# Two output projections of a transformer kernel: three matmuls per weight tile become two, one of them 512 columns wide

## The reference, cut to what matters

```python
for l in range(DEPTH_2):
    x = x + hybrid_mixer(rms_norm(x, norm_mix[l]), w_in[l], ..., w_out[l], rows, cos, sin)
    x = x + memory_cross_attention(rms_norm(x, norm_mem_q[l]), rms_norm(mem, norm_mem_kv[l]), ...)
    x = x + conv_ffn(rms_norm(x, norm_ffn[l]), w_up[l], conv_w[l], conv_b[l], w_down[l])
return rms_norm(x, norm_final)
```

## Time and profile before

| | |
|---|---|
| median of 3 runs | 2555.58 us (2552.3 to 2555.68) |
| profiled execution, its own time | 2551.63 us |
| its span | 2549.8 us |
| mean granted TensorE clock | 0.962 |
| busy: TensorE, VectorE, ScalarE, POOL | 92%, 61%, 48%, 24% |
| matmuls from L729 with rounded weights | 6688 + 3424 + 3424 + 1632, 275 to 300 ns each in flight |
| DMA | 342.94 MB, 134 GB/s on average |

### The profile page before, as it was taken

One profiled execution on the slowest core, in us unless ns is written; L12 is line 12 of the kernel. 1 busy time (PEld: TensorE's weight loads), 2 busy tenths in 40 slices (PEclk: granted clock), 3 DMA queues, 4 the chain that ended last, 5 costly groups with the idle time before them and its releaser, 6 DMA issues. The chain is left out here.

```text
span 2549.8 us, 47516 instructions
## 1 busy us (share of the span) xinstructions
PE 2338.9 (92%) x19162; PEld 2195.9 (86%) x19162; DVE 1566.3 (61%) x2510; ACT 1215.1 (48%) x1859; POOL 621.2 (24%) x744
## 2 busy tenths in 40 slices
PE   4999999899999898799989899996898998889998
PEld 3888999798998687699977789995698998778998
DVE  4665654645654665465546656546667975656994
ACT  4455544444543642455345554443445554444653
POOL 3114211013211030032121132213174540053550
PEclk8889999999999999899999999998999999989999
DMA  4223545323555221155442245453243554233554
GB/s 160 84 83 133 180 154 189 123 83 122 176 162 169 100 68 51 51 168 179 155 144 84 90 136 173 160 189 121 83 163 120 189 165 166 67 119 130 189 171 136
DMA packets 52715, 342.94 MB, mean 134 GB/s; under 512 B 5888, under 2 KB 7104, under 8 KB 20160
## 3 DMA queue, kind: packets, MB, share of 16 engines
q1 hardware_dynamic: 51984, 336.26, 39.9%
q0 software_dynamic: 560, 4.26, 0.4%
HBM read 339.38 MB, written 1.05 MB: 134 GB/s over the span
## 5 line engine op out<-in xcount | busy, mean ns | idle before, releaser
L729 PE MATMUL ps<-arena_r,ring_hi 128*128 128x272 f32 (+1 forms) x6688 | 1605.5, 289 | 15.6 <-DVE arena L2107 7.4
L729 PEld LDWEIGHTS ps<-arena_r,ring_hi 128*128 128x128 f32 x6688 | 1178.2, 192 | 19.9 <-DVE arena L2107 7.8
L729 PE MATMUL ps<-y_r,ring_hi 128*128 128x272 f32 (+1 forms) x3424 | 1024.5, 299 | 22.7 <-POOL arena_r L2843 10.2
L1983 DVE TENSOR_TENSOR ring_lo<-ring,ring_hi 128x2048 fp32r<-128x2048 f32 (+1 forms) x348 | 737.8, 2121 | 411.8 <-ACT ring_hi L1461 411.0
L729 PE MATMUL ps<-y_r,ring_lo 128*128 128x272 f32 (+1 forms) x3424 | 989.1, 289 | 0.0
L729 PEld LDWEIGHTS ps<-y_r,ring_hi 128*128 128x128 f32 x3424 | 659.8, 193 | 59.1 <-issue 25.6
L1461 ACT ACTIVATE ring_hi<-ring 128x2048 fp32r<-128x2048 f32 (+1 forms) x348 | 607.5, 1747 | 121.9 <-DMA ring<-dn 49.9
L729 PEld LDWEIGHTS ps<-y_r,ring_lo 128*128 128x128 f32 x3424 | 661.7, 193 | 0.0
L729 PE MATMUL ps<-arena_r,ring_lo 128*128 128x272 f32 (+1 forms) x1632 | 469.2, 287 | 0.0
L729 PEld LDWEIGHTS ps<-arena_r,ring_lo 128*128 128x128 f32 x1632 | 311.3, 191 | 0.0
L1461 ACT ACTIVATE arena<-arena 128x272 f32<-128x272 f32 (+7 forms) x199 | 93.4, 472 | 409.5 <-DVE arena L2538 268.8
(11 more groups left out here) (229 smaller groups left out, 1725.8 us busy)
## 6 DMA issues: line engine op xcount, KB each, us to landing
ring<-gu SPq DMA_DIRECT2D x88, 1024.0 KB, 5.0
ring<-dn SPq DMA_DIRECT2D x64, 704.0 KB, 4.0
ring<-up SPq DMA_DIRECT2D x44, 1024.0 KB, 5.1
ring<-fox_in SPq DMA_DIRECT2D x32, 1024.0 KB, 5.1
ring<-sdn SPq DMA_DIRECT2D x32, 704.0 KB, 4.0
ring<-gdn_in SPq DMA_DIRECT2D x16, 1024.0 KB, 5.1
ring<-in SPq DMA_DIRECT2D x16, 1024.0 KB, 5.1
ring<-gla_in SPq DMA_DIRECT2D x12, 1024.0 KB, 5.1
```

Of the source, the lines that this page charges most:

```text
L729: return nc.tensor.matmul(dst, w, mv, start=start, stop=stop)
L1983: V.tensor_tensor(ring_lo[:, slot, 0:w], ring[:, slot, 0:w], ring_hi[:, slot, 0:w].bitcast(F32), ALU.subtract).then_inc(lo_ready, 1)
```

## The change

The input of a chunk becomes one view of its high and its low part, 2 x 256 columns (h2_both_r, a_both_r), and one matmul takes both through the high weights into a PSUM tile of 512 columns, which is a whole bank. The low weights by the high input go as a second matmul of 256 columns to the first half of that tile. In sdn the high input lies first in memory, so the first half collects both products of the high input and the second half high weights by low input; in out2 the low part lies first, so the halves are the other way round for the wide matmul. Each tile thus holds two partial sums of 256 columns, and residual() adds first the one half to x, waits for that, then adds the other. This holds for out2_0, out2_1, sdn0 and sdn1. No other stage, no transfer and no weight split changes.

```diff
--- before.py
+++ after.py
@@ -525,6 +525,7 @@
         h1_r, h1_lo_r = view_r(0, FC, T), view_r(7104, FC, T)
         h2_r, h2_lo_r = view_r(5120, FC, SEQ), view_r(10752, FC, SEQ)
         y_lo_r, y_lo2_r = view_r(18304, KC, T), view_r(18176, KC, SEQ)
+        h2_both_r, a_both_r = view_r(5120, 2, FC, SEQ), view_r(14080, 2, KC, SEQ)
         a_hi_r, a_o_r = view_r(16128, KC, SEQ), view_r(14080, KC, SEQ)
         m_lo_r, m_y_r, m_hi_r = view_r(7168, KC, SEQ), view_r(11264, KC, SEQ), view_r(17152, 4, SEQ)
 
@@ -728,7 +729,7 @@
             def mm(dst, w, mv, start=True, stop=True):
                 return nc.tensor.matmul(dst, w, mv, start=start, stop=stop)
 
-            def blocks(nb, tpb, kc, src, width, ready, after=None, banks=BANKS, middle=None):
+            def blocks(nb, tpb, kc, src, width, ready, after=None, banks=BANKS, middle=None, double=False):
 
 
 
@@ -750,10 +751,15 @@
                                 pe.wait_ge(lo_ready, i * (2 * turn) + (2 * (n.block + b) + half + 1))
                             hi, lo = ring_hi[:, slot, at:at + P], ring_lo[:, slot, at:at + P]
                             shi, slo = src(k)
-                            dst = acc(n.tile + t, width, P, banks)
-                            mm(dst, hi, shi, k == 0, False)
-                            mm(dst, hi, slo, False, False)
-                            last = mm(dst, lo, shi, False, k == kc - 1)
+                            if double:
+
+                                mm(acc(n.tile + t, 2 * SEQ, P, banks), hi, shi, k == 0, False)
+                                last = mm(acc(n.tile + t, SEQ, P, banks), lo, slo, False, k == kc - 1)
+                            else:
+                                dst = acc(n.tile + t, width, P, banks)
+                                mm(dst, hi, shi, k == 0, False)
+                                mm(dst, hi, slo, False, False)
+                                last = mm(dst, lo, shi, False, k == kc - 1)
                             if tpb == 1 and k == kc // 2 - 1:
                                 last.then_inc(mid_ready, 1)
                             if middle is not None and k == kc // 2 - 1:
@@ -964,13 +970,13 @@
                 all_read()
                 n.out += KC
 
-            def project_out(nb, tpb, kc, src, width, chunks, late):
+            def project_out(nb, tpb, kc, src, width, chunks, late, double=False):
                 def ready(k):
                     if k >= late:
                         pe.wait_ge(late_split, n.late + k - late + 1)
                     else:
                         pe.wait_ge(out_split, n.split + k + 1)
-                blocks(nb, tpb, kc, src, width, ready)
+                blocks(nb, tpb, kc, src, width, ready, double=double)
                 n.split += late
                 n.late += chunks - late
                 new_norm(width)
@@ -1427,7 +1433,7 @@
                     blocks(nb, tpb, kc, y_parts2, SEQ, y_chunk)
                     n.pair += FC
                 elif name.startswith("sdn"):
-                    blocks(nb, tpb, kc, lambda k: (h2_r[:, k, :], h2_lo_r[:, k, :]), SEQ, lambda k: pe.wait_ge(h_split, n.pair - FC + k + 1))
+                    blocks(nb, tpb, kc, lambda k: (h2_both_r[:, :, k, :], h2_r[:, k, :]), SEQ, lambda k: pe.wait_ge(h_split, n.pair - FC + k + 1), double=True)
                     new_norm(SEQ)
                 elif name.startswith("dn"):
                     w = SEQ if name == "dn3" else T
@@ -1436,7 +1442,7 @@
                 elif name.startswith("in2"):
                     hybrid(name, nb, tpb, kc)
                 elif name.startswith("out2"):
-                    project_out(nb, tpb, kc, lambda k: (a_hi_r[:, k, :], a_o_r[:, k, :]), SEQ, KC, KC)
+                    project_out(nb, tpb, kc, lambda k: (a_both_r[:, :, k, :], a_hi_r[:, k, :]), SEQ, KC, KC, double=True)
                 elif name.startswith("memkv"):
                     memory(name, nb, tpb, kc)
                 elif name.startswith("memq"):
@@ -2013,12 +2019,17 @@
                     v.wait_ge(sqsum_ready, n.norm * KC + c)
                     V.tensor_tensor(sqsum[:, 0:width], sqsum[:, 0:width], sq[:, c % 2, 0:width], ALU.add).then_inc(sqsum_ready, 1)
 
-            def residual(dst, width, norm_width, hook, short):
+            def residual(dst, width, norm_width, hook, short, double):
 
                 for c in range(KC):
                     if short:
                         hook(c)
-                    V.tensor_tensor(dst[:, c, :], take(c, width), dst[:, c, :], ALU.add).then_inc(evacuated, 1)
+                    if double:
+
+                        step(V.tensor_tensor(dst[:, c, :], take(c, 2 * SEQ)[:, 0:SEQ], dst[:, c, :], ALU.add))
+                        V.tensor_tensor(dst[:, c, :], take(c, 2 * SEQ)[:, SEQ:2 * SEQ], dst[:, c, :], ALU.add).then_inc(evacuated, 1)
+                    else:
+                        V.tensor_tensor(dst[:, c, :], take(c, width), dst[:, c, :], ALU.add).then_inc(evacuated, 1)
                     if not short:
                         hook(c)
                     if c:
@@ -2723,7 +2734,7 @@
                     n.out += 4
                 if name in GAINS:
                     second = name.startswith(("out2", "memo", "sdn"))
-                    residual(xs if second else x, SEQ if second else T, SEQ if second or name == "dn3" else T, after, tpb == 1)
+                    residual(xs if second else x, SEQ if second else T, SEQ if second or name == "dn3" else T, after, tpb == 1, name.startswith(("out2", "sdn")))
                     if name == "dn3":
 
                         V.memset(u_gp[:, :, 0:1], 0.0)
```

## The result

The changed kernel takes 2557.9 us (median of 22 runs, 2552.28 to 2568.61), the kernel before 2552.41 us (22 runs, 2541.86 to 2556.59). The ratio is 1.0025, with a 95% interval from 1.0013 to 1.0036: slower by a quarter of a per cent, a little more than the 0.2% that the prediction took as its bound, which the interval includes. The forecast was a gain of 0.14%. The time lies inside the range (2547 to 2558), by a hair; the direction was wrong.

What follows compares the result with a forecast made beforehand. TensorE's matmul spacing was taken to bound out2 and sdn. 4.5 us saved there less 0.9 us lost in two tails gave -3.6 us, from the median 2555.58 to 2552.0 us (-0.14%), range 2547 to 2558.

Steps and rivals of the forecast that it cites:

- The bound: In out2 and sdn TensorE's matmul spacing is the time: 117.8 ns per 256 columns in sdn, 353.4 per step.
- A gap per matmul and not per column: In out2 and sdn, wide matmul takes its columns plus one 11.1 ns gap, 224.4 ns; a step saves 11.1.
- rival 1: In out2 and sdn the gap is per column: wide matmul 235.6 ns, saved 0, 2556.5 us; chance 0.24.
- The 4.5 us saved: TensorE in out2 and sdn: 402 paying steps x 11.1 ns = 4.5 us saved.
- Rival 2: In out2 and sdn the wide matmul hides the next weight load: 215.6 ns, 2548.5 us; chance 0.15.
- Rival 3: In out2 and sdn the wide matmul is dearer than two: 243 ns, +3.9 us, 2559.5 us; chance 0.10.
- Steps that don't pay: Of 480 steps, 12 at out2's 1.2 GHz starts, 44 in sdn's second tiles, 22 at sdn0's end save nothing.
- Inside the stages it is covered.: In out2 and sdn the added 0.46 us of VectorE per tile is hidden; out2 busy about 16.3 of 20.35 us.
- bound for lost cover: In out2, if cover were gone, a tile would cost up to 0.46 us, 7 us over 16 tiles.
- After out2, memkv works on other data for 22 us and hides it.: Behind out2, the last tile's later residual costs nothing, since memkv runs on other data for 22 us.
- Two tails: At the ends of sdn0 and sdn1 the second addition is exposed: 2 x 0.46 = 0.9 us lost.
- The sum: Whole kernel: -4.5 + 0.9 = -3.6 us, giving 2552.0 us, -0.14%; forecast's chance 0.47.

Runs made afterwards that it cites:

- e7: Kernel before with 224 instead of 256 columns in every sdn matmul, one execution, trace only: matmuls start 111.7 ns apart.
- e6: Kernel before with the sum-of-squares matmul moved behind memkv's third tile, one execution, trace only: memkv0 27.06, memkv1 25.27 us.
- e10: Kernel before with the edits of e6 and e9 together: ratio 1.0044 (1.0028 to 1.0060).
- e13: As e9 on the kernel before, but the second half of the split also waits for POOL's last y step: 2549.04 against 2553.49 us, 0.9985 (0.9970 to 0.9999).
- e2: Changed kernel with the wide matmul but one VectorE addition per tile, second half left out of the sum: 2552.25 us, ratio 0.9993 (0.9977 to 1.0010).
- e11: Kernel before with two idle extra VectorE additions at every out2 tile, one execution, trace only: memkv0 28.81, memkv1 28.52 us.
- e1: Kernel before, three matmuls kept, with an idle second VectorE addition per tile in out2 and sdn: 2558.09 against 2551.0 us, ratio 1.0023 (1.0010 to 1.0036).
- e3: Kernel before with the change made in out2 alone, sdn as before: 2555.51 us, ratio 1.0014 (0.9999 to 1.0028).
- e8: Changed kernel with sdn's wide matmul reading 512 adjacent columns, low input left out, one execution, trace only: seven sdn1 tiles 54.66 us.
- e9: Kernel before, last residual and sums put ahead of the second half of the next weight split in one-tile-per-block stages: ratio 1.0001 (0.9989 to 1.0014).

## Why the prediction was wrong, point by point

- **The bound.** Right for the time inside the stages: TensorE's matmuls bound out2 and sdn, before and after. But behind TensorE in out2 stood a loop of VectorE and ScalarE that was slower than it even before, and the prediction did not see it.
- **"A gap per matmul and not per column", 224.4 ns for the wide matmul.** Wrong. It takes 233.4, and the narrow one behind it 120.0: rival 1 (twice the old matmul, nothing saved) holds to a tenth of a nanosecond per step. The 4.5 us saved were 402 times a gap that one instruction less does not remove. The rows had both readings, 1.066 against 1.063 for a rate, and I chose by the 0.9 ns that up0 lies lower. Rival 2 fell with it: a wide matmul over the next load took 233.4 ns and not 215.6. The Trainium skill (TensorE: Matmul & The Clock Gate, LDWEIGHTS) gives a load the time of its columns over 1.2, 106.7 ns for 128 columns, an estimate from that page; the 111.7 ns in e7 lie near it, and no run here shows that the load sets them. Rival 3 fell too, the slope of 0.49 ns per column did not carry to 512. What the 11.1 ns are stays open: in sdn1 of e6, e10 and e13 they are 6.7, with the same matmuls.
- **Steps that don't pay** (start at 1.2 GHz, second tile, end of sdn0). They never mattered, since no step paid.
- **"Inside the stages it is covered."** Wrong, and this makes the loss. The busy time of VectorE in out2 was about as forecast (15.3 of 20.4 us at the full clock in the changed kernel, 16.3 of 20.35 forecast), and it hid nothing: what counted was the turn-taking of two queues, VectorE's and ScalarE's, 5.85 us per two tiles before and 6.31 after, where TensorE needs 5.65. I named who stands behind the residual and did not add up their chain. The prediction had a bound for lost cover, 7 us over out2's 16 tiles, and gave it no place in the sum and no rival of its own.
- **"After out2, memkv works on other data for 22 us and hides it."** Wrong in its place: TensorE's queue holds the sum of squares behind memkv's first tile, 3 us after out2, not 22. These two steps together are 1.81 + 2.22 us in memkv, of which 0.8 to 1.1 and 2.2 are left at the next sdn, where the sum had nothing.
- **Two tails, 0.9 us.** Right after sdn1, 0.46 us by the traces. After sdn0 the two traces differ by 0.1 us, which is less than such traces differ by themselves. The times resolve neither.
- **The sum.** 0 saved, 3.0 to 3.3 us lost behind out2, 0.6 in tails: 3.6 to 3.9 us by the traces. The medians give 5.5, the ratio 6.4 with an interval from 3.3 to 9.2. The traces reach only its lower end; what the rest is, a share of the clock or chance, stays open. That the time fell into the range at all is luck: two steps were wrong, and rival 1's 2556.5 us, from which the upper end was drawn, had no loss in memkv. Slower by over 0.2% had a chance of 0.08, since all mechanisms for it but a dearer wide matmul were taken as covered.

## What to carry to other kernels

A busy share of 64% (VectorE in out2 before) says nothing about cover where two in-order engines release each other tile by tile: add up one round of their chain (who waits for whom, in queue order) and compare that with the time of the engine that should bound. For a stage's last product, look in the bounding engine's own queue for the first entry that needs it; that entry, and not the next stage that reads it, sets how late it may be. And before fewer, wider matmuls are bought with work elsewhere, run the wide matmul by itself, as e2 does: two widths 16 columns apart left both readings open, and e2 decides it.

## What the runs showed of the hardware

- Rounded (float32r) matmuls at the 2.4 GHz level started 0.456 to 0.462 ns per column apart at 256, 272 and 512 columns, where the clock alone gives 0.417; at the 1.2 GHz level 256 columns took 213.3 ns, exactly the clock's, and fp32 matmuls of 272 columns at 2.4 GHz took 229 ns, where twice the columns are 226.7. At 224 columns the spacing was 111.7 ns. In sdn1 of three traces (e6, e10, e13) 256 columns took 113.4 ns instead of 117.8. What limits the spacing, and what chooses between these two, is not shown by any run here.
- Joining two matmuls of 256 columns on the same weights into one of 512 left the step at 353.4 ns (233.4 + 120.0 against 3 x 117.8).
- After a TensorE wait of 3.8 us in memkv0 of e11 (3.7 in memkv1) the granted clock was 0.50 for 3.41 us; after waits of 1.5 to 2.2 us in after, e1 and e3 it stayed at 1.00, and after one of 2.19 us in e8 it fell for 3.41 us.
- A POOL step of 0.48 us took 2.51 us when it began just after a VectorE subtraction of two 2048-column operands of 2.29 us, and 0.48 us again when it was kept apart; TensorE's wait behind it was 2.31 us in e9 and 0.34 in e13. The Trainium skill (SBUF — State Buffer, two separate sides) has VectorE with two SBUF inputs and POOL take one port pair in turn, whole instructions at a time. These traces agree: in e9 the POOL step ended 0.35 us after the subtraction.
